# Two transformer blocks on one core: the last expert group's down pieces cut by output half, the PLE gate product begun on one half, and the latent products of the second mixer in rounded parts

## The chip, the core and the metric

The program runs on one core of a Trainium2 chip. The core has TensorE (PE, matmuls into PSUM; PEld is its weight load), VectorE (DVE), ScalarE (ACT), GpSimd (POOL), SyncE (SP, which here only issues DMAs) and 16 DMA engines. Each engine runs its own list of instructions in order; they meet at semaphores. The metric is the time of one execution on the device, in microseconds, and the median of some runs stands for a kernel. Lower is better.

## What is computed

256 tokens of width 1024 pass through two blocks. The first is a mixer and a convolutional MLP. The second is what the change is about:

```python
def second_block(x, p, ...):
    h = _rmsnorm(x, norm_mix_g)
    c_q, c_kv, k_r, x_m, z, i_pre, f_pre = _split_in(h @ w_in)
    q = (_rmsnorm(c_q, q_norm_g) @ w_uq)        # 256 -> 8 heads x 96
    kv = (_rmsnorm(c_kv, kv_norm_g) @ w_ukv)    # 128 -> 8 heads x (64 + 64)
    attn_out = _mla_attention(...)
    xc = silu(_causal_conv(x_m, conv_w, conv_b))
    mq, mk, mv = ...                            # per-head products of xc, xc and x_m
    hm = _mlstm_chunkwise(mq, mk, mv, ig, fg)   # gates from i_pre and f_pre, scanned over time
    ml_out = (norm(hm) + ml_skip * xc) * silu(z)
    x = x + concat([attn_out, ml_out]) @ w_o
    x = x + _hier_moe(_rmsnorm(x, norm_ffn_g), ...)  # 32 experts, top 2 of one group of 8
    hp = _rmsnorm(x, norm_ple_g)
    x = x + (p @ w_ple) * sigmoid(hp @ w_ple_gate)
    return _rmsnorm(x, final_norm_g)
```

An expert is `(silu(x @ w_g) * (x @ w_u)) @ w_d` with an inner width of 256.

## The kernel before

**Exact products.** A product in full float32 is one `pe.matmul`, which the trace records as two. Elsewhere both operands are cut into a rounded high part (ACT casts it) and a rounded remainder (one subtraction), and `product` (L1853) issues three matmuls: high by high, high by low, low by high.

**The second mixer.** PE first turns the normed rows (`turn_h`, L1840) and multiplies them by the 424 columns of the latents and gates (L2122, float32). Then come four column tiles of x_m and, after the transposes of the latents (`cT`), of the rope terms and of the gates, four of z (`tiles`, L2128, rounded parts, 24 matmuls a tile). The high parts of z come from ACT (L962), the remainders from POOL (L676). The gate rows are scanned on DVE (L1502 to L1505) on 4 partitions. PE turns and spreads them (L2168), then makes q from the latents (L2180, float32), k (L2188) and v (L2194), then mq (L2209) and the attention scores (L2221). In the meantime DVE makes the four convolutions of x_m (L1514 to L1518), the weights' arguments (L1527, L1529) and the turned half of q (L1536). ACT evacuates q, k and v and rounds the eight pieces of w_o (L943) between them; POOL lowers those pieces (L685). The second half of w_o is loaded only when z is done, since it takes the panel's place (L539, semaphore `zw_used`). The raw latent weights lie in `W`; chunk 0 of the expert weights is loaded to `spare` before they are used.

**The experts.** 32 experts go in 8 groups of 4. Each group has six chunks of 2 MB, four of up weights and two of down weights, which SP loads to a ring of 12 places in the order of use; a place is loaded again when PE has used it. Per group (`pe_step`) PE gathers tokens (L2426), makes the up product (L2442), puts the rows of the step before back to their tokens (`scatter`, L2448, four matmuls a token block: two output halves, high and low), turns the activation (L2489) and makes the down product (L2502). A down chunk holds one half of the inner width for both output halves (banks 2 and 3), so both halves are complete only with the second chunk. After the last group come `last_scatter`, the two gate panels of 2 MB each, `turn_x(4, ...)` (L2363), the gate product for half 0 of block 0 in float32 (`gate_full`, L2549) and three more in rounded parts (`gate_product`). ACT and DVE close: sigmoid, product, sum, norm, store.

## Time and profile before

| | us |
|---|---|
| median of 3 runs (673.68 to 674.1) | 673.91 |
| the profiled execution | 672.95 |
| its span in the trace | 671.1 |
| PE busy | 628.6 (94%) |
| DVE busy | 377.3 (56%) |
| ACT busy | 279.6 (42%) |
| the chain that ended last: PE, DMA | 70%, 18% |

The span is what the trace covers; 1.85 us of the profiled execution lie around it. Busy shares are means over stages that have different limits: up to some 530 us PE is nearly always busy, from there to 632 us PE waits for weights again and again, and after the last chunk the DMA engines fall idle. The mean granted clock of PE is 0.985 of full speed.

### The profile page before, as it was taken

The numbers are of one execution on the slowest core, as the hardware profiler recorded it, in microseconds if no ns is written. First come the engines' busy times: TensorE is split into PE (matmuls) and PEld (weight loads), VectorE is DVE, ScalarE is ACT, GpSimd is POOL, SyncE is SP. The second block draws the span as 40 slices with busy tenths as digits, with TensorE's granted clock in tenths as the row PEclk, the third lists the DMA queues.
The fourth block names the chain that finished last, engine by engine and source line by source line (L and its number), as shares of the span: only waits on it lengthen the run. The fifth ranks groups of instructions, "written<-read, shape, count | busy, mean of one in ns | idle before, by whom it ended". The sixth has DMA issues, their size and how long they took to land.

```text
span 671.1 us, 11002 instructions
## 1 busy us (share of the span) xinstructions
PE 628.6 (94%) x4299; PEld 478.6 (71%) x4299; DVE 377.3 (56%) x665; ACT 279.6 (42%) x434; POOL 55.7 (8%) x82
## 2 busy tenths in 40 slices
PE   8999999999999999999999999999999986768895
PEld 5999998889999999996796888644444432325364
DVE  5596967587677777776777465542233221203195
ACT  6764375566555555556946721311101100010193
POOL 3000000300000000200093600000000000000010
PEclk9999999999999999999999999999999998898998
DMA  8933542777655555204923658999899999999931
GB/s 328 371 136 135 201 133 68 270 259 236 212 188 188 188 187 183 69 1 161 390 92 126 211 194 303 370 426 430 352 432 427 428 424 430 426 425 427 406 124 63
DMA packets 54604, 174.81 MB, mean 260 GB/s; under 512 B 4774, under 2 KB 29474, under 8 KB 48162
## 3 DMA queue, kind: packets, MB, share of 16 engines
q1 hardware_dynamic: 53888, 172.54, 67.3%
q10 hardware_dynamic: 674, 1.69, 0.7%
q8 instruction: 30, 0.49, 0.3%
q14 instruction: 12, 0.10, 0.0%
HBM read 173.17 MB, written 1.05 MB: 260 GB/s over the span
## 4 chain that ended last, share of the span: by engine, by line
PE 70%; DMA 18%; DVE 5%; ACT 4%; issue 2%; ACTq 0%; another core or an unknown queue 0%; POOLq 0%; POOL 0%; DVEq 0%; PEldq 0%
PE ps L1855 15%; PE ps L1857 14%; PE ps L1856 14%; DMA spare<-in_w_moe_dram 7%; DMA W<-in_w_moe_dram 7%; PE ps L2442 6%; PE ps L2426 3%; PE ps L2502 3%; PE ps L2448 2%; PE ps L2122 2%; DMA W<-in_w_in_dram 2%; DMA W<-in_w_o_dram 1%; PE ps L2549 1%; PE ps L2270 1%; DMA arena<-in_conv_ffn_dram 1%
## 5 line engine op out<-in xcount | busy, mean ns | idle before, releaser
L1855 PE MATMUL ps<-hT_high,w_up_parts 128*128 128x256 f32 x320 | 90.8, 284 | 0.0
L1857 PE MATMUL ps<-hT_high,w_up_parts 128*128 128x256 f32 x320 | 90.6, 283 | 0.0
L1856 PE MATMUL ps<-hT_low,w_up_parts 128*128 128x256 f32 x320 | 90.5, 283 | 0.0
L1344 DVE TENSOR_TENSOR w_up_parts<-W,w_up_parts 128x1024 fp32r<-128x1024 f32 x44 | 52.4, 1222 | 22.7 <-ACT w_up_parts L848 22.7
L1855 PEld LDWEIGHTS ps<-hT_high,w_up_parts 128*128 128x128 f32 x320 | 61.4, 192 | 0.5
L1856 PEld LDWEIGHTS ps<-hT_low,w_up_parts 128*128 128x128 f32 x320 | 61.4, 192 | 0.4
L1857 PEld LDWEIGHTS ps<-hT_high,w_up_parts 128*128 128x128 f32 x320 | 61.4, 192 | 0.0
L1038 ACT ACTIVATE sg<-ps 128x256 f32<-128x256 f32 x9 | 3.5, 384 | 121.1 <-PE ps L2442 121.1
L2442 PE MATMUL ps<-W,junk 128*32 128x512 f32 x368 | 46.1, 629 | 7.5 <-DMA W<-in_w_moe_dram 7.5
L848 ACT CAST w_up_parts<-W 128x1024 fp32r<-128x1024 f32 x44 | 44.5, 1048 | 20.4 <-PE ps L1857 20.4
L1855 PE MATMUL ps<-h_high,dense_high 128*128 128x256 f32 x160 | 45.8, 286 | 0.6 <-DVE dense_low L1219 0.4
L1856 PE MATMUL ps<-h_low,dense_high 128*128 128x256 f32 x160 | 45.3, 283 | 0.0
L1857 PE MATMUL ps<-h_high,dense_low 128*128 128x256 f32 x160 | 45.2, 283 | 0.0
L2426 PEld LDWEIGHTS ps<-arena,x_tok 128*128 128x128 f32 x288 | 35.3, 204 | 11.0 <-issue 11.0
L1367 DVE SCALAR_TENSOR_TENSOR arena<-ps,arena 128x255 f32<-128x255 f32 x80 | 33.1, 476 | 17.2 <-ACT arena L884 16.9
L2426 PE MATMUL ps<-arena,x_tok 128*128 128x128 f32 x288 | 36.9, 290 | 3.1 <-DVE arena L1712 2.0
L1219 DVE TENSOR_TENSOR dense_low<-W,dense_high 128x1024 fp32r<-128x1024 f32 x31 | 36.0, 1218 | 2.7 <-ACT dense_high L777 2.6
L777 ACT CAST dense_high<-W 128x1024 fp32r<-128x1024 f32 x30 | 29.4, 1044 | 13.0 <-PE ps L1857 10.0
L2442 PEld LDWEIGHTS ps<-W,junk 128*32 128x32 f32 x368 | 10.7, 112 | 31.1 <-issue 20.7
L1855 PE MATMUL ps<-w_down_high,uact_high 128*128 128x512 f32 x80 | 31.4, 392 | 0.9 <-DVE uact_low L1378 0.9
L1855 PEld LDWEIGHTS ps<-h_high,dense_high 128*128 128x128 f32 x160 | 30.6, 192 | 2.0 <-issue 1.5
L1856 PE MATMUL ps<-w_down_low,uact_high 128*128 128x512 f32 x80 | 31.3, 391 | 0.0
(491 smaller groups left out, 1346.6 us busy)
## 6 DMA issues: line engine op xcount, KB each, us to landing
W<-in_w_moe_dram SPq DMA_DIRECT2D x22, 2048.0 KB, 21.1
arena<-in_w_moe_dram SPq DMA_DIRECT2D x14, 2048.0 KB, 30.1
W<-in_w_up_dram SPq DMA_DIRECT2D x22, 1024.0 KB, 8.2
W<-in_w_in_dram SPq DMA_DIRECT2D x7, 2048.0 KB, 10.4
W<-in_w_down_dram SPq DMA_DIRECT2D x11, 1024.0 KB, 4.9
spare<-in_w_moe_dram SPq DMA_DIRECT2D x5, 2048.0 KB, 20.7
hh<-in_w_moe_dram SPq DMA_DIRECT2D x4, 2048.0 KB, 33.1
W<-in_w_out_dram SPq DMA_DIRECT2D x2, 2048.0 KB, 8.7
```

Of the source, the lines that this page charges most:

```text
L777: act.copy(piece(panel_hl(n)[0], n, c), piece(panel(n), n, c)).then_inc(sig("dense_high"), 1)
L848: act.copy(w_up_hl[0][:, c], U[q][:, :, g, i * P:(i + 1) * P]).then_inc(sig("up_high"), 1)
L1219: dve.tensor_tensor(piece(panel_hl(n)[1], n, c), piece(panel(n), n, c), piece(panel_hl(n)[0], n, c).bitcast(F32), ALU.subtract).then_inc(s ...
L1344: dve.tensor_tensor(w_up_hl[1][:, c], U[q][:, :, g, i * P:(i + 1) * P], w_up_hl[0][:, c].bitcast(F32), ALU.subtract).then_inc(sig("up_low" ...
L1367: dve.scalar_tensor_tensor(o, s, w, o, ALU.mult, ALU.add).then_inc(sig("tap_done"), 1)
L1855: pe.matmul(o, lhs[0], rhs[0], start=first, stop=False, skip_group_check=True)
L1856: pe.matmul(o, lhs[0], rhs[1], start=False, stop=False, skip_group_check=True)
L1857: return pe.matmul(o, lhs[1], rhs[0], start=False, stop=last_k, skip_group_check=True)
L2122: last = pe.matmul(ps[:, 2 + b, 0:424], hT[:, k, b * P:(b + 1) * P], wA[:, k, :], start=(k == 0), stop=(k == KD - 1))
L2426: last = pe.matmul(ps[:, h, (k % 4) * P:(k % 4 + 1) * P], x_tok[:, b, k * P:(k + 1) * P], hot[:, b, :], start=(b == 0), stop=(b == 1))
L2442: last = pe.matmul(ps[CAP * c:CAP * c + CAP, 2, :], xg[:, k, CAP * c:CAP * c + CAP], up_chunk(CPG * g + j)[:, c, kk, :], start=(k == 0), s ...
L2502: last = pe.matmul(ps[CAP * c:CAP * c + CAP, bank, :], aT[:, f, CAP * c:CAP * c + CAP], down_chunk(CPG * g + UPC + f)[:, c, 512 * half:512 ...
```

## The change

**Last group and gate.** The host lays the down weights out anew: each of the two down chunks of a group now holds one output half for the whole inner width. All groups compute one half, then the other (`down_half`), and ACT rounds the first half's rows after the first chunk. In the last group the first half is put back to its tokens before the last quarter of the down product (`scatter_half`, twice: for the rows of the step before it stands ahead of the last group). The last chunk is loaded in two parts of 1 MB, cut by inner half, and the first gate panel too, with rows 4 to 7 of its eight first; the gate weights are laid out in one piece. The gate product of block 0 begins on the turned rows of half 1 (k = 4 to 7) while half 0 is put back. Ten short matmuls (`keep_sharp`) stand in the last group in place of five of 512 columns.

**Second mixer.** The latents and their weights are rounded (ACT, four casts) and lowered (DVE, four subtractions), and q, k and v use `product`. The remainders of z move from POOL to DVE. The gate rows are turned, and half of them spread, between the third and the fourth tile of z. The convolutions are cut in two pairs around the weights' arguments. POOL starts the pieces of w_o after the last convolution. Chunk 0 is loaded later, with chunk 1, since `spare` now holds rounded weights.

**End of the first MLP.** POOL instead of DVE lowers one of the last down pieces; the down products of the last pairs stand in another order, the last one of the first token block two products further ahead; DVE evacuates two turned halves earlier in the hand-over; 6 of 10 filler matmuls go.

```diff
@@ SP
-            load_chunk(0)
             sp.wait_ge(sig("a2_used"), 1)
             sp.dma_start(PAN[5], w_o[:, :, 512:1024]).then_inc(sig("wo1_landed"), 16)
...
             sp.wait_ge(sig("uq_used"), 1)
+            load_chunk(0)
             load_chunk(1)
...
+                elif n == NCHUNK:
+                    sp.dma_start(ring(n)[:, 0:UNIT // 2], w_moe[NGRP8 - 1, CPG - 1][:, 0:UNIT // 2]).then_inc(sig("last_landed"), 16)
+                    sp.dma_start(ring(n)[:, UNIT // 2:UNIT], w_moe[NGRP8 - 1, CPG - 1][:, UNIT // 2:UNIT])\
+                        .then_inc(sig(f"ring{n % RING}_landed"), 16)
+                elif n == NCHUNK + 1:
+                    sp.dma_start(wpg[0][:, 4:KD, :], w_gate[0, :, 4:KD, :]).then_inc(sig("gate_landed"), 16)
+                    sp.dma_start(wpg[0][:, 0:4, :], w_gate[0, :, 0:4, :]).then_inc(sig(f"ring{n % RING}_landed"), 16)
@@ POOL
-            for c in range(4):
-                o = (slice(None), slice(None), slice(c * P, c * P + P))
-                pool.wait_ge(sig("dense_high"), 32 + 4 + c + 1)
-                pool.tensor_tensor(z_low[o], PAN[1][o], proj_high[:, c].bitcast(F32), ALU.subtract).then_inc(sig("dense_rest"), 1)
...
+            pool.wait_ge(sig("conv2_late"), at("conv2_late", 2))
             for n, (h, q) in enumerate(WO_PARTS):
@@ ACT
+            act.wait_ge(sig("cT_ready"), at("cT_ready", 2))
+            act.copy(cT_hl[0], cT).then_inc(sig("ct_high"), 1)
+            act.wait_ge(sig("uq_landed"), at("uq_landed", 32))
+            for j in range(3):
+                raw, high, _ = latent_piece(j)
+                act.copy(high, raw).then_inc(sig("lat_high"), 1)
             round_out(WO_PARTS[0:2])
...
+            for n in range(2):
+                conv, xc, qn = (("conv2_done", "xc_ready", "qn_ready"), ("conv2_late", "xc_late", "qn_late"))[n]
+                for h in (2 * n, 2 * n + 1):
+                    act.wait_ge(sig(conv), at(conv, h - 2 * n + 1))
+                    act.activation(xcT[:, h, :], xcT[:, h, :], ACT.Silu, bias=par_c("conv_b_2", h)).then_inc(sig(xc), 1)
+                for hp in (2 * n, 2 * n + 1):
+                    act.wait_ge(sig("qa_done"), at("qa_done", hp + 1))
+                    act.mul(qTa[0:64, 2 * hp:2 * hp + 2, :], v3(ps[0:64, hp, :], 2), A_SCALE).then_inc(sig(qn), 1)
+                    if hp < 3:
+                        round_out(WO_PARTS[2 + hp:3 + hp])
@@ PE
-            keep_busy(0, 4)
+            keep_busy(0, 3)
             turn_h(2, 0)
-            keep_busy(3, 6)
+            keep_busy(3, 1)
...
+            tiles(z_low, (2, 3), "dense_rest", 0, ("z2_done", "z2_late"), turn_gates)
+            pe.wait_ge(sig("z2_late"), at("z2_late", 1))
+            pe.sem_inc(sig("zw_used"), 1)
+            spread_max(1)
...
-                        last = pe.matmul(ps[:, hp, 256 * hh:256 * hh + 256], uq[:, k, h * P:(h + 1) * P], cT[:, k, :],
-                                         start=(k == 0), stop=(k == 1))
+                        last = product(ps[:, hp, 256 * hh:256 * hh + 256], [t[:, k, h * P:(h + 1) * P] for t in uq_hl],
+                                       [t[:, k, :] for t in cT_hl], k == 0, k == 1)
...
+            def expert_down(n, g):
+
+                pe.wait_ge(sig("aT_ready"), n + 2)
+                down_half(n, g, 0).then_inc(sig("downw_used"), 1)
+                if g < NGRP8 - 1:
+                    down_half(n, g, 1).then_inc(sig("downw_used"), 1)
+                    return
+                pe.wait_ge(sig("sc_ready"), n + 2)
+                keep_sharp(6)
+                down_half(n, g, 1, (0,))
+                scatter_half(n + 1).then_inc(sig("half_back"), 1)
+                keep_sharp(4)
+                down_half(n, g, 1, (1,)).then_inc(sig("downw_used"), 1)
...
+            turn_ple(1)
+            pe.wait_ge(sig("ypa_ready"), begun + 1)
+            for b in range(TB):
+                slots_back(b, 0, False)
+            turn_ple(3)
+            gate_full(4)
+            pe.wait_ge(sig("yl_ready"), begun * 2 + 2)
+            for b in range(TB):
+                slots_back(b, 0, True).then_inc(sig("moe_done"), 1)
+            gate_full(5)
+            gate_full(6)
+            turn_ple(0)
+            gate_full(7)
+            turn_ple(2)
+            for k in range(3):
+                gate_full(k)
+            gate_full(3).then_inc(sig("pg_done"), 1)
@@ DVE
...
+            dve.wait_ge(sig("half_back"), at("half_back", rounds))
+            for b in range(TB):
+                dve.tensor_copy(x_tok[:, b, 512:D], ps[:, 5 + 2 * b, :]).then_inc(sig("x_ready"), 1)
+            turned_ple(1)
+            lower_slots(0, begun)
+            turned_ple(3)
+            dve.wait_ge(sig("moe_done"), 1)
+            dve.tensor_copy(x_tok[:, 0, 0:512], ps[:, 4, :]).then_inc(sig("x_ready"), 1)
+            lower_gate(2)
+            turned_ple(0)
...
```

On PE at the end of the last group, before: `hh` and `spare` hold the two down chunks, `sg` the activation, `slots_high` and `slots_low` the rounded rows, `scatter_rows` the map back to the tokens; a count stands for matmuls alike in a row.

```order
L2502 MATMUL ps<-hh,sg 32x512 x8
L2498 MATMUL ps<-slots_high 128x512 x5
L2502 MATMUL ps<-spare,sg 32x512 x8
L2536 REGISTER_ALU
L2536 COMPARE_AND_BRANCH
L2538 TENSOR_LOAD arena
L2538 ISA x2
L2463 REGISTER_ALU
L2448 MATMUL ps<-slots_high,scatter_rows 128x512 x4
L2470 ISA
L2448 MATMUL ps<-slots_low_67,scatter_rows 128x512
```

There, after:

```order
L2585 MATMUL ps<-hh,sg 32x512 x8
L2606 MATMUL ps<-scatter_rows 128x256 x6
L2585 MATMUL ps<-spare,sg 32x512 x4
L2536 MATMUL ps<-slots_high,scatter_rows 128x512 x2
L2557 ISA
L2536 MATMUL ps<-slots_low_67,scatter_rows 128x512 x2
L2606 MATMUL ps<-scatter_rows 128x256 x4
L2585 MATMUL ps<-spare,sg 32x512 x4
```

Eight matmuls on the last chunk have become four and four, with the rows of one half put back between them. Behind them PE had the 4 turns, the last rows back and the gate product one after the other; now 4 turns of half 1, the rows of half 0 and single gate matmuls alternate.

On DVE in the second mixer, from the transposed latents (L1494) to the first convolution (L1514), before; the four rows on 4x256 are the scan of the gates:

```order
L1494 TENSOR_TENSOR arena<-ps,par 128x3x128 x2
L1498 COPY arena<-ps 64x256
L1499 COPY arena<-ps 64x256
L1500 COPY arena<-ps 4x512
L1502 SCALAR_TENSOR_TENSOR arena<-arena 4x256
L1503 TENSOR_TENSOR arena<-arena 4x256
L1504 SCALAR_TENSOR_TENSOR arena<-arena 4x256
L1505 TENSOR_TENSOR arena<-arena 4x256
L1514 TENSOR_SCALAR arena<-arena,par 128x256
L1516 SCALAR_TENSOR_TENSOR arena<-arena,par 128x256 x2
```

There, after:

```order
L1530 TENSOR_TENSOR z_low<-W,proj_high 128x8x128 x2
L1537 TENSOR_TENSOR arena<-ps,par 128x3x128 x2
L1530 TENSOR_TENSOR z_low<-W,proj_high 128x8x128
L1542 COPY arena<-ps 64x256
L1543 COPY arena<-ps 64x256
L1544 COPY arena<-ps 4x512
L1530 TENSOR_TENSOR z_low<-W,proj_high 128x8x128
L1547 SCALAR_TENSOR_TENSOR arena<-arena 4x256
L1548 TENSOR_TENSOR arena<-arena 4x256
L1549 SCALAR_TENSOR_TENSOR arena<-arena 4x256
L1550 TENSOR_TENSOR arena<-arena 4x256
L1553 TENSOR_TENSOR cT_low<-arena,cT_high 128x768
L1557 TENSOR_TENSOR latent_low<-W,latent_high 128x2x512 x2
L1557 TENSOR_TENSOR latent_low<-W,latent_high 128x1024
```

The four subtractions of z stand around the evacuations, and the four of the latents between the scan and the convolutions.

## Rows read from the trace of the kernel before

**Rows 1.** windows: busy us by engine, granted clock, DMA share, GB/s of stretches.

```profile
368.10:380.30 12.20, 11.79 (x75) 10.13 (x73) 5.95 (x13) 10.55 (x18) 8.91 (x4) 1.00 0.48 174
...
478.00:480.00 2.00, 2.00 (x24) 0.52 (x16) 0.00 (x0) 0.00 (x0) 0.00 (x0) 1.00 0.60 139
...
490.00:500.00 10.00, 10.00 (x90) 5.47 (x90) 3.76 (x7) 1.07 (x2) 0.00 (x0) 1.00 1.01 429
...
570.00:580.00 10.00, 8.93 (x64) 5.33 (x64) 3.33 (x6) 1.07 (x2) 0.00 (x0) 0.83 1.00 426
...
636.00:638.00 2.00, 1.68 (x8) 0.94 (x7) 1.41 (x3) 1.02 (x3) 0.00 (x0) 1.00 1.06 388
```

**Rows 2.** the chain that ended last: start us, us, what.

```profile
352.94 8.89 DMA W<-in_w_o_dram
...
583.81 48.65 DMA spare<-in_w_moe_dram
```

**Rows 3.** timeline, PE, 312 to 339 us: start, us, line, names, [idle before].

```profile
312.23 1.09 PE L1850 MATMUL ps<-ident,hh 128*128 128x128 f32 x8 [0.91 <-DVE hh L1191]
...
314.46 4.50 PE L2122 MATMUL ps<-W,hh 128*128 128x424 f32 x12
...
327.35 0.36 PE L1855 MATMUL ps<-h_high,proj_high 128*128 128x256 f32 x1 [0.40 <-PE ps L2122]
...
338.93 0.82 PE L2144 MATMUL ps<-ident,arena 128*128 128x128 f32 x6
```

**Rows 4.** timeline, PE, the second mixer, 353 to 371 us.

```profile
353.36 1.97 PE L2168 MATMUL ps<-arena 4*128 4x256 f32 x8
...
355.26 7.17 PE L2180 MATMUL ps<-arena,W 128*128 128x256 f32 x32
...
363.01 3.67 PE L2188 MATMUL ps<-arena,W 128*64 128x256 f32 x16 [0.58 <-DVE arena L1529]
...
370.81 5.40 PE L2221 MATMUL ps<-arena 128*128 128x128 f32 x32
```

**Rows 5.** timeline, DVE and then POOL, 342 to 353 us.

```profile
342.85 2.89 DVE L1502 TENSOR_TENSOR_SCAN arena<-arena 4x256 f32<-4x256 f32 x1
...
350.34 2.45 DVE L1505 TENSOR_TENSOR arena<-arena 4x256 f32<-4x256 f32 x1
...
347.30 5.21 POOL L685 TENSOR_TENSOR wo_low<-W,wo_high 128x1024 fp32r<-128x1024 f32 x2
```

**Rows 6.** groups by line, DVE: names, shapes, count | busy us, mean ns.

```profile
L1241 DVE TENSOR_TENSOR_SCAN arena<-arena 128x512 f32<-128x512 f32 x1 | 1.2, 1226 | 0.0
...
L1219 DVE TENSOR_TENSOR dense_low<-W,dense_high 128x1024 fp32r<-128x1024 f32 x31 | 36.0, 1218 | 2.7 <-ACT dense_high L777 2.6
```

**Rows 7.** timeline, ACT, 361 and 380 us.

```profile
361.85 1.04 ACT L943 CAST wo_high<-W 128x1024 fp32r<-128x1024 f32 x1 [0.74 <-DMA W<-in_w_o_dram]
...
380.31 0.75 ACT L1001 CAST nm<-ps 8x256 fp32r<-8x256 f32 x2
```

**Rows 8.** timeline, PE, last group and gate products, from 627 us.

```profile
627.80 1.92 PE L2502 MATMUL ps<-hh,sg 128*32 128x512 f32 x16
...
632.50 1.92 PE L2502 MATMUL ps<-spare,sg 128*32 128x512 f32 x16 [1.42 <-DMA spare<-in_w_moe_dram]
...
635.22 1.18 PE L2448 MATMUL ps<-slots_high,scatter_rows 128*128 128x512 f32 x4 [0.80 <-ACT slots_high L1042]
...
639.26 3.67 PE L2549 MATMUL ps<-W,hh 128*128 128x512 f32 x8 [0.44 <-DVE hh L1639]
...
643.64 3.60 PE L2549 MATMUL ps<-W,hh 128*128 128x512 f32 x8
...
646.68 0.79 PE L1855 MATMUL ps<-wpg_high,hpT_high 128*128 128x512 f32 x1
...
663.20 0.39 PE L1857 MATMUL ps<-wpg_high,hpT_low 128*128 128x512 f32 x1
```

**Rows 9.** timeline, DVE, near the end of the program.

```profile
664.40 0.69 DVE L1811 TENSOR_TENSOR arena<-arena 128x512 f32<-128x512 f32 x1 [1.77 <-ACT arena L1078]
```

More of the change, by code:

```diff
@@ L1759, in _ @@
                 if g == NGRP8 - 1:
+                    lower_slots(1, begun)
                     for q in range(4):
@@ L1838, in _, with turn_h @@
             keep_busy(4, 6)
-            def turn_h(r, b):
-                for h in range(2):
+            def turn_h(r, b, halves=range(2)):
+                for h in halves:
                     j = 2 * b + h
@@ L2126, in _, with tiles @@
             pe.sem_inc(sig("a2_used"), 1)
-            def tiles(low, banks, ready, base, signal):
+            def tiles(low, banks, ready, base, signals, between=None):
                 for h in range(2):
@@ L2187, in _ @@
                     h = 2 * hp + hh
-                    last = pe.matmul(ps[0:NOPE, 4 + hp, 256 * hh:256 * hh + 256], ukv[:, h * P:h * P + NOPE], cT[:, 2, :],
-                                     start=True, stop=True)
+                    last = product(ps[0:NOPE, 4 + hp, 256 * hh:256 * hh + 256], [t[:, h * P:h * P + NOPE] for t in ukv_hl],
+                                   [t[:, 2, :] for t in cT_hl], True, True)
                 last.then_inc(sig("ka_done"), 1)
@@ L2563, in _ @@
[L2563 to L2569 removed]
+                        pe.wait_ge(sig("y1_low"), 7 + HP_ORDER.index(2 * b + k // 4) + 1)
+                    last = product(ps[:, 5 + 2 * b - half, :], [t[:, k, b * P:(b + 1) * P] for t in hpT],
+                                   [wpg_high[half][:, k, :], wpg_low[half][:, k, :]], k == ks[0], k == ks[-1])
```

424 lines of the change are left out of this document (236 added, 188 removed).

## The prediction, made before the changed kernel was run

> **What bounds the kernel now.** I read the chain of waits first, then the windows, then the timelines at the places where the chain changes hands. The chain ends with the weight stream: the load of the last chunk to `spare` (48.65 us in a full queue, landed at 632.5) and then 38.6 us of work behind it up to the end of the span at 671.1 [rows 2, 8]. Before the stream the chain runs through the second mixer, and there it holds the load of half of w_o, 8.89 us from 352.94, which can start only when z is done [rows 2]. In between lie the groups. The windows say who leads there: at 478 to 480 us PE is busy all the time and the DMA share falls to 0.60, since the ring is full and SP waits for a place; from 490 us on the share is 1.01 [rows 1]. So the stream restarts when PE frees a place near 479 us and is full from then on: what the mixer gains or loses before that point moves the stream, and with it the landing at 632.5, one for one. What happens on PE between 490 and 627 us moves nothing. The sum therefore has two parts: the mixer's exit, and the work behind the last landing.
>
> **The change, part by part. 1, the way into the mixer.** Two products of the last down stage are moved behind the last one of token block 0. A rounded matmul of 512 columns takes 0.233 us (71 steps from 646.68 to 663.20) [rows 8], so this block's result comes 6 x 0.233 = 1.4 us earlier, less 0.2 us in which PE now waits for the activation remainder of DVE: 1.2. The b0 turns stood waiting on DVE until 312.23 [rows 3] and go to 311.1. Between their end (1.09 us later) and the first latent product at 314.46 stood six fillers; with one, the product can start when DVE has evacuated the first half, about 0.2 us after the turns, at 312.4. The 16 latent products and the other turns are as many as before, so the x_m tiles start at 325.3 for 327.35: **2.0 us earlier**. Cover: the rounding of x_m must be ready at 325.3; ACT and DVE do it in the same order from rows that are turned 1 us earlier, so some tenths may be lost.
>
> **2, the gates.** On DVE the scan's four rows reach from 342.85 to 350.34 + 2.45 = 352.8, 9.9 us. A scan over 512 columns takes 1.2 us elsewhere [rows 6], here one over 256 takes 2.89, and a subtraction of 256 columns 2.45 [rows 5]. The last subtraction starts inside POOL's two pieces of w_o and ends at 352.8, just after they do at 347.30 + 5.21 = 352.5. I read this as DVE held up until POOL's instruction is over. Without a neighbour the four take about 2 x 0.65 + 2 x 0.3 = 1.9 us (an estimate: half of 1.2 each for the scans). The change takes POOL's pieces away until the convolutions are done and adds 4 x 1.22 us of z on DVE [rows 6], of which two stand in an idle stretch, one behind the turned latents, and the last before the scan, where it may wait for POOL's copy. I get gates at 345.2; PE asks for them after the third z tile at 347.7. Cover 2.5 us. If the 9.9 us stay, they come after 352 and PE stands some 2 to 5 us with a z tile behind the wait.
> In the Trainium skill, page SBUF — State Buffer, section SBUF: two separate sides, the pair of ports that VectorE and GpSimd share is an exclusive lock for a whole instruction, also for a VectorE operation with two SBUF inputs against GpSimd. The rows agree, but the rule cuts the other way too. The eight w_o pieces (2.6 us each, half of 5.21 [rows 5]) now run in one row after the last convolution, over the small minimum behind the scores; by the rule it can wait up to 2.6 us, and the sum would then end 0 to 1.5 us worse.
>
> **3, q, k and v.** A rounded matmul of 256 columns takes (338.93 - 327.35) / 96 = 0.121 us [rows 3]. For q 32 records of 7.17 us become 48 x 0.121 = 5.8; for k 3.67 becomes 24 x 0.121 = 2.9 [rows 4]; for v two float32 products of 512 columns (0.92 each, as 3.67 for four [rows 8]) become 6 x 0.233 = 1.4. Together 2.6 us less PE. The price: three casts of 1.04 and a smaller one on ACT [rows 7], and about 4.6 us on DVE (3.8 x 1.22) ahead of the convolutions. DVE has them done at 349.6 and the first two convolutions at 353.3, for 356.4 in the old order.
>
> **4, where that gain goes.** z ends at 350.9 + 1.0 (turning and half of the 1.97 us of spreading [rows 4] now stand in it) = 352.0, so the w_o half is asked for 0.95 us earlier, and q starts at 352.9 for 355.26: 2.35 earlier. q ends at 358.75, k at 361.7. But ACT, in order, rounds a w_o piece after its first share of q. It waited 0.74 us for the load at 361.85 [rows 7]; now it waits there from 355.0 to 360.9. Behind it stand the second share of q (v waits for it), two more convolutions' silu, two pieces, the other q and k: about 7.4 us, to 368.3. The scores need k from ACT, so they start at 368.3 for 370.81 [rows 4]: 2.5 earlier, with PE idle some 3 us in between. From there ACT has the same list as before and no idle time left: between 368.1 and 380.3 it was busy for 10.55 of 12.2 us [rows 1], so 1.6 us idle, and the row maxima's cast at 380.31 [rows 7], on which the next step hangs, stands at the end. So that point moves by 1.3 us only. **The mixer's exit: 1.3 us earlier.** Bounds: 2.5 if ACT's list lies beside the path after all; a loss of 0.9 if the gates keep their 9.9 us, by the same walk. I take 1.3 since that is what the busiest queue allows. The later load of chunk 0 costs nothing: two chunks are 10 us from 364, and SP asks for the next only at about 378.
>
> **5, behind the last landing.** L is the landing, 632.5. Before: down 1.92, wait 0.80, four rows back high (1.18) and four low, turns, two float32 halves of 3.67 and 3.60 at 639.26 and 643.64, then 72 rounded matmuls from 646.68, which is L + 14.2 [rows 8]. After: only a quarter of the down product needs the last megabyte, 0.96. Rows back of half 1 (four of eight, 1.1) are done before L; PE is at 632.3 with them if the first megabyte comes 2.4 us before the second (half of the 4.9 us that a chunk takes at 429 GB/s [rows 1]). What remains before the 72: 0.96 + two pairs of rows back 1.1 + four turns of 0.5 + float32 7.3 = 11.4, and the waits for ACT and DVE now have a turn or a gate matmul beside them; the gate panel's first half must be there at L + 2.4, asked for at L + 3. So they start at L + 11.4 to 11.6: 2.7 us earlier on PE, at most 3.1. DVE is the second limit: its eight remainders of the gate (9.8 us), four of the turned rows and the evacuations fill it until about L + 20.4, and PE's last two products need them at a distance of 0 to 0.2 us. The closing chain hangs on DVE's row at 664.40, which waited 1.77 us [rows 9]; I get it at 661.6. **2.8 us earlier.** Bounds: 1.0 if the parts do not land ahead (then only the rows back of half 1 leave the path), 3.4 if every wait goes. The gate weights in one piece should also lift the 388 GB/s at 636 to 638 [rows 1] towards 429, which nobody waits for.
>
> **The sum.** 671.1 - 1.3 - 2.8 = 667.0 for the span, 672.95 - 4.1 = 668.85 for the profiled execution. That one lies 0.96 under the median of 673.91, and I carry the difference: 673.91 - 4.1 = **669.8 us**.
>
> **Rivals.** *A, the mixer gives nothing* (ACT's list, or 0.5 us here and there): for it speak 3 us of new idle time on PE and a load that ACT must wait for 5.9 us; 671.1. *B, both give all*: 2.5 and 3.4, 668.0. *C, the change does not do what it says at the end*: the first part of the last chunk lands with the second, since both lie in one full queue on 16 engines; then PE waits for it, and the tail gives 1.0: 671.6, or 672.9 with a mixer that gives nothing. *D, slower, by the clock.* PE ran at 0.83 mean in 570 to 580, at work for 8.93 of 10 us and waiting for DMA [rows 1]; that is the 1.2 GHz level for a third of the time. After the change PE works in shorter pieces between waits behind L, and the fillers are shorter. If the clock falls to 1.2 GHz for all of the float32 gate part, its 7.3 us become 14.6 and the time 677. It decides from 4.1 us on, more than half of that part. Against it: 1.00 at 636 to 638, where PE worked 1.68 of 2 us [rows 1].
> The Trainium skill, TensorE: Matmul & The Clock Gate, section HAM oscillation, has it that matmuls in bursts between waits for DMA fall back to the lower level again and again. By it D would be likelier than I hold it.
>
> **Chances.** Forecast (668.9 to 670.8) 0.50; A 0.22; B 0.12; C 0.10, of which 0.06 within 0.2% of the old time; D 0.04; the rest lies between. 0.2% is 1.35 us, about what a measurement of this kernel can tell from no change. The range of 8 in 10 takes in B and A and the better half of C: 667.8 to 672.2. Faster 0.90, same 0.06, slower 0.04.
>
> **What would show it.** In the new trace: the x_m tiles start near 325.3; the four scan rows take about 2 us; q starts near 352.9; the scores near 368.3, the row maxima's cast near 379.0; the last down quarter starts where its DMA ends, near 631.2 (L itself moved by 1.3); the first rounded gate matmul 11.5 us after it for 14.2. The prediction is wrong if the stream is not tied to PE near 479 us (then the tail alone shows), if PE stands before the last z tile, or if the granted clock is under 0.95 after the last landing.

## The result, and the profile after

The changed kernel takes 668.3 us (median of 4 runs, 667.8 to 668.4), for 674.0 us before in the same series. The ratio is 0.992 (95% interval 0.990 to 0.993): 5.7 us less. The profiled execution took 668.31 us with a span of 666.6, for 672.95 and 671.1 before. So the two profiles differ by 4.6 us and the medians by 5.7; the forecast was 4.1 for both. Two of the eight executions of `pool_back`, an experiment below, were in a much slower state (1027 and 1568 us) and are left out of its ratio.

The load of the w_o half still stands on the chain of waits, about where it stood [rows 2]. The last load on the chain is now that of the first down chunk (`hh`), since the last chunk no longer holds PE up:

```profile
352.84 8.97 DMA W<-in_w_o_dram
...
581.33 44.65 DMA hh<-in_w_moe_dram
```

PE's timeline from the mixer's entry to the scores answers to [rows 3, 4]; start us, us, line, names, idle time before:

```profile
325.77 0.36 PE L1930 MATMUL ps<-h_high,proj_high 128*128 128x256 f32 x1 [0.30 <-PE ps L2198]
...
348.28 0.41 PE L2249 MATMUL ps<-ident,arena 4*128 4x4 f32 x4
348.55 1.10 PE L2238 MATMUL ps<-arena 4*128 4x256 f32 x4
...
352.87 1.10 PE L2238 MATMUL ps<-arena 4*128 4x256 f32 x4
...
369.08 5.48 PE L2309 MATMUL ps<-arena 128*128 128x128 f32 x32 [0.87 <-ACT arena L1012]
```

The x_m tiles start 1.58 us earlier than in [rows 3], the scores 1.73 us earlier than in [rows 4]. The gate rows on DVE, which reached from 342.85 to 352.8 [rows 5], are over in 2.3 us:

```profile
343.32 0.67 DVE L1547 TENSOR_TENSOR_SCAN arena<-arena 4x256 f32<-4x256 f32 x1
344.03 0.41 DVE L1548 TENSOR_TENSOR arena<-arena 4x256 f32<-4x256 f32 x1
344.47 0.68 DVE L1549 TENSOR_TENSOR_SCAN arena<-arena 4x256 f32<-4x256 f32 x1
345.19 0.41 DVE L1550 TENSOR_TENSOR arena<-arena 4x256 f32<-4x256 f32 x1
```

ACT's timeline answers to [rows 7]. It stands at the w_o half for 5.60 us where it stood for 0.74, and it goes on at the same time, 361.83 for 361.85. Yet the row maxima's cast comes 1.64 us earlier, because ACT has no idle time left behind the load (1.6 us of it before, in five waits for PE between 371 and 380 us):

```profile
355.63 0.59 ACT L1007 ACTIVATE arena<-ps 64x512 f32<-64x512 f32 x1 [1.49 <-PE ps L1932]
361.83 1.05 ACT L969 CAST wo_high<-W 128x1024 fp32r<-128x1024 f32 x1 [5.60 <-DMA W<-in_w_o_dram]
...
366.92 2.02 ACT L1012 COPY arena<-ps 64x512 f32<-64x512 f32 x4
...
378.67 0.74 ACT L1035 CAST nm<-ps 8x256 fp32r<-8x256 f32 x2
```

The two parts of the last chunk, by the view of one tile (issue, then the least, median and longest time to landing), land at 582.38 + 46.1 = 628.5 and 594.09 + 36.8 = 630.9. The second is the landing L, 1.6 us earlier than before:

```profile
L602 SPq DMA_DIRECT2D spare<-in_w_moe_dram x1: 11670/11670/11670, 582.4 to 582.4; - x1
L603 SPq DMA_DIRECT2D spare<-in_w_moe_dram x1: 2404/2404/2404, 594.1 to 594.1; - x1
...
DMA to landing us min/median/max: 36.8/41.5/46.1
```

PE at the close, and DVE's row that waited at 664.40 before [rows 8, 9]:

```profile
628.87 1.06 PE L2585 MATMUL ps<-spare,sg 128*32 128x512 f32 x8
...
630.90 0.64 PE L2606 MATMUL ps<-scatter_rows 128*128 128x256 f32 x4
631.46 1.07 PE L2585 MATMUL ps<-spare,sg 128*32 128x512 f32 x8
...
642.04 0.80 PE L1930 MATMUL ps<-wpg_high,hpT_high 128*128 128x512 f32 x1
...
659.86 0.69 DVE L1886 TENSOR_TENSOR arena<-arena 128x512 f32<-128x512 f32 x1
```

The first rounded gate product stands at L + 11.1 (L + 14.2 before), the end of the span at L + 35.7 (L + 38.65 before). PE's granted clock is 1.00 from 630 to 645. The gate panels move at 429 and 442 GB/s (631 to 634 and 634 to 637 us), where it had been 388 [rows 1].

### The profile page after: what moved, and what is told of

Read it like the earlier page. It is cut to its first block, busy times and chain, and to the rows that moved or that the text cites. A ratio compares the mean times of both kernels' runs of the same rounds, so it can differ in the third digit from the quotient of the medians.

```text
span 666.6 us, 11072 instructions
## 1 busy us (share of the span) xinstructions
PE 623.8 (94%) x4324; PEld 476.4 (71%) x4324; DVE 379.3 (57%) x673; ACT 282.1 (42%) x437; POOL 48.8 (7%) x79
## 4 chain that ended last, share of the span: by engine, by line
PE 62%; DMA 17%; DVE 8%; ACT 7%; SPq 3%; issue 2%; ACTq 0%; POOLq 0%; POOL 0%; DVEq 0%; PEldq 0%
PE ps L1930 13%; PE ps L1932 13%; PE ps L1931 13%; DMA hh<-in_w_moe_dram 7%; DMA W<-in_w_moe_dram 6%; PE ps L2530 6%; PE ps L2514 3%; PE ps L2585 3%; SPq L553 3%; PE ps L2198 2%; DMA W<-in_w_in_dram 2%; PE ps L2536 2%; DMA W<-in_w_o_dram 1%; PE ps L2358 1%; DMA arena<-in_conv_ffn_dram 1%
## 5 line engine op out<-in xcount | busy, mean ns | idle before, releaser
L874 ACT CAST w_up_parts<-W 128x1024 fp32r<-128x1024 f32 x44 | 44.5, 1048 | 20.3 <-PE ps L1932 20.3
L2514 PEld LDWEIGHTS ps<-arena,x_tok 128*128 128x128 f32 x288 | 32.8, 192 | 8.4 <-issue 8.4
L2514 PE MATMUL ps<-arena,x_tok 128*128 128x128 f32 x288 | 34.4, 278 | 1.5 <-ACT x_tok L1060 0.9
## 6 DMA issues: line engine op xcount, KB each, us to landing
W<-in_w_in_dram SPq DMA_DIRECT2D x7, 2048.0 KB, 10.7
```

Source lines behind the costliest of these rows:

```text
L874: act.copy(w_up_hl[0][:, c], U[q][:, :, g, i * P:(i + 1) * P]).then_inc(sig("up_high"), 1)
L2514: last = pe.matmul(ps[:, h, (k % 4) * P:(k % 4 + 1) * P], x_tok[:, b, k * P:(k + 1) * P], hot[:, b, :], start=(b == 0), stop=(b == 1))
```

## Milestones of all runs

The experiments are read by five points of each trace. The profiled executions differ by up to 0.8 us before anything of the change is reached (the first block's turns on PE start between 114.2 and 115.0), so distances say more than times. A distance has a spread of its own: five kernels with the same mixer code (after, tail_mixer, no_fillers, one_piece, filler_late) have mixers of 52.54 to 53.13. "Mixer" is from the first x_m tile to the row maxima's cast, "stream" from there to L, "tail" from L to the span's end. Ratios are to the kernel before of the same series.

| kernel | x_m tiles | mixer | stream | tail | span | ratio (interval) |
|---|---|---|---|---|---|---|
| before | 327.35 | 52.96 | 252.1 | 38.7 | 671.1 | |
| after | 325.77 | 52.90 | 252.2 | 35.7 | 666.6 | 0.992 (0.990 to 0.993) |
| tail_only | 327.58 | 54.00 | 252.5 | 35.6 | 669.7 | 0.996 (0.995 to 0.998) |
| tail_mixer | 327.72 | 52.72 | 252.0 | 35.7 | 668.1 | 0.994 (0.993 to 0.995) |
| latents_f32 | 325.63 | 52.54 | 252.4 | 35.7 | 666.3 | 0.992 (0.991 to 0.994) |
| wo_behind | 326.06 | 50.01 | 252.5 | 35.8 | 664.4 | 0.987 (0.986 to 0.989) |
| gates_behind | 325.40 | 52.74 | 252.3 | 35.6 | 666.0 | 0.990 (0.988 to 0.991) |
| pool_back | 325.51 | 60.80 | 253.1 | 35.6 | 675.0 | 1.004 (1.003 to 1.006) |
| before_again | 327.46 | 52.95 | 252.1 | 38.7 | 671.2 | |
| no_fillers | 325.55 | 53.04 | 252.5 | 35.2 | 666.3 | 0.990 (0.988 to 0.992) |
| one_piece | 325.58 | 53.13 | 252.2 | 39.4 | 670.3 | 0.996 (0.994 to 0.997) |
| filler_late | 325.26 | 52.54 | 252.1 | 35.8 | 665.7 | 0.992 (0.990 to 0.993) |
| both_f32 | 325.97 | 52.59 | 252.2 | 35.7 | 666.5 | 0.992 (0.991 to 0.993) |
| best | 325.41 | 49.99 | 252.2 | 35.2 | 662.8 | 0.987 (0.986 to 0.989) |

The stream's column is the first finding: over exits that range from 375.4 to 386.3 it stays at 252.0 to 253.1 (252.0 to 252.5 without `pool_back`). What the mixer gains or loses reaches the landing nearly one for one.

## The experiments

**The change in its parts.** `tail_only` is the kernel before with the expert weights' layout, the last group and the gate product of the change; `tail_mixer` has the second mixer's edits too. What is then missing to the changed kernel is the end of the first MLP. These lines, from the changed kernel to `tail_mixer`, show the order of the down products and the fillers:

```diff
...
-            down_before(1, 0, range(1))
+            down_before(1, 0, range(2))
+            down_before(1, 1, range(1))
             down_last(0, 1).then_inc(sig("y_done"), 1)
...
-            keep_busy(0, 3)
+            keep_busy(0, 4)
             turn_h(2, 0)
-            keep_busy(3, 1)
+            keep_busy(3, 6)
...
```

> The kernel before with the change of the last group, of the expert weights' layout and of the gate product alone; mixer and first MLP as before. Theory (two separate parts, the second is the work behind the last landing): the last chunk lands where it did, near 632.4, the first rounded gate product comes about 11.2 us behind it (14.2 before), the span is 671.1 - 2.9 = 668.2, the ratio to before 0.9957. Rival (the tail needs the earlier mixer, or the extra microsecond by which the medians moved more than the two profiled executions lies in the tail): span 669.5 or more in the one case, ratio 0.994 in the other.

> The changed kernel with the end of the first MLP and the hand-over to the second mixer as before (fillers, order of the last down products, DVE lowering both pieces). Theory (the mixer's exit hangs on the end of z, the load of the w_o half behind it and ACT's list behind that load, so it keeps only what z's end keeps): x_m tiles at 327.35, z's end and the load 1.5 us later than in the changed kernel (352.84), the cast of the row maxima at 380.2 (378.67 in the changed kernel, 380.31 before); the mixer's own edits then give 0.1 us and the time is that of tail_only within 0.3 us. Rival (the mixer's own edits give most of the 1.64 us and the earlier start the rest, as the forecast had it that DVE's and PE's savings count by themselves): cast at 379.3 or earlier, 1 us or more under tail_only.

Measured: medians 671.5 us and 669.9 us, for 674.0 before and 668.3 after. The tail is 3.0 to 3.1 us shorter in both, as in the changed kernel: it needs nothing of the mixer. That part of the theory holds, but the span of `tail_only`, 669.7, is on the rival's side (669.5 or more), for a reason that neither had named: 1.0 us in its mixer, below. In `tail_mixer` the mixer takes 52.72 us for 52.96 before. ACT's timeline there shows why: the load is later by the tiles' later start, the wait is as long as in the changed kernel, and the cast is back at its old place.

```profile
363.60 1.05 ACT L966 CAST wo_high<-W 128x1024 fp32r<-128x1024 f32 x1 [5.45 <-DMA W<-in_w_o_dram]
...
380.44 0.74 ACT L1032 CAST nm<-ps 8x256 fp32r<-8x256 f32 x2
```

So by the traces the mixer's own edits gave next to nothing (52.54 to 53.13 in the five kernels that have them, 52.95 and 52.96 in the two traces of the kernel before), the MLP's end 1.8 us (first x_m tile against the turns at 114 us: 212.9 before, 211.1 after), the tail 3.0 us. The medians don't divide like that: from `tail_only` to `tail_mixer` they fall by 1.6 us, where the theory had 0.3 at most and only the rival 1 or more, although the cast, at 380.44, is the theory's (380.2) and not the rival's (379.3). The windows of `tail_only` (us, busy of PE, PEld, DVE, ACT, POOL, granted clock, DMA share, GB/s) show what is missing:

```profile
352.00:356.00 4.00, 3.69 (x23) 2.92 (x23) 3.82 (x8) 1.10 (x2) 0.74 (x1) 0.97 0.36 97
356.00:360.00 4.00, 4.00 (x13) 3.24 (x12) 3.75 (x10) 1.02 (x2) 0.00 (x0) 0.61 1.05 400
```

Its mixer is the code of before, and yet takes 54.00 us for 52.96: the clock fell to about the 1.2 GHz level for some 3 us, just behind the turned and spread gates, and q got slower. I come back to that under `gates_behind`.

**Do the rounded latents pay?** `latents_f32` makes q, k and v from the raw weights again and drops the four casts and the four remainders:

```diff
...
-                        last = product(ps[:, hp, 256 * hh:256 * hh + 256], [t[:, k, h * P:(h + 1) * P] for t in uq_hl],
-                                       [t[:, k, :] for t in cT_hl], k == 0, k == 1)
+                        last = pe.matmul(ps[:, hp, 256 * hh:256 * hh + 256], uq[:, k, h * P:(h + 1) * P], cT[:, k, :],
+                                         start=(k == 0), stop=(k == 1))
...
```

> The changed kernel with q, k and v made in float32 from the raw latents again, no casts and remainders for them. Theory (ACT's list behind the w_o load sets the exit, PE has idle time there): PE busy 2.6 us more between 352 and 369, the cast of the row maxima stays within 0.2 us of 378.67, the time within 0.3 us of the changed kernel (668.3). Rival (q, k and v lie on the path): exit and time 1.5 to 2.6 us later, 670 to 671.

Measured: 668.05 us (one of its five executions took 670.27), ratio 0.992, mixer 52.54 us for 52.90. The windows of 352 to 369 us, first of this kernel, then of the changed one:

```profile
352.00:369.00 17.00, 16.44 (x73) 11.72 (x73) 7.61 (x16) 9.64 (x18) 6.72 (x3) 1.00 0.47 145
```

```profile
352.00:369.00 17.00, 14.38 (x96) 12.07 (x95) 10.46 (x25) 9.15 (x17) 7.12 (x3) 1.00 0.51 178
```

In this stretch PE has 2.06 us more work (2.6 were expected) and 2.06 us less idle time, and nothing behind it gets later: the cast comes at 378.17 for 378.67. In the changed kernel the rounded latents are worth nothing.

**The wait that takes it.** `wo_behind` lets ACT round the late pieces of w_o behind what PE waits for:

```diff
...
-                for hp in (2 * n, 2 * n + 1):
-                    act.wait_ge(sig("qa_done"), at("qa_done", hp + 1))
-                    act.mul(qTa[0:64, 2 * hp:2 * hp + 2, :], v3(ps[0:64, hp, :], 2), A_SCALE).then_inc(sig(qn), 1)
-                    if hp < 3:
-                        round_out(WO_PARTS[2 + hp:3 + hp])
+            silu_conv(0)
+            for hp in range(4):
+                act.wait_ge(sig("qa_done"), at("qa_done", hp + 1))
+                act.mul(qTa[0:64, 2 * hp:2 * hp + 2, :], v3(ps[0:64, hp, :], 2), A_SCALE).then_inc(sig(("qn_ready", "qn_late")[hp // 2]), 1)
+            silu_conv(1)
...
                 act.wait_ge(sig("mq_done"), at("mq_done", h + 1))
                 act.copy(mqT[:, 2 * h:2 * h + 2, :], v3(ps[:, 2 + h, :], 2)).then_inc(sig("mq_ready"), 1)
+            round_out(WO_PARTS[2:4])
...
```

> The changed kernel with ACT's roundings of the w_o pieces moved behind the evacuations: q, k, v and mq first, then two pieces, the exponentials, two pieces, and the last two behind the cast of the row maxima. Theory (the exit hangs on ACT standing at the load of w_o until 361.83 with q and k behind it): no such wait ahead of k, scores near 366.0 for 369.08, cast of the row maxima at 376.5 to 377, time 1.7 to 2.2 us under the changed kernel, 666.3. Rival (something else, DVE's maxima, POOL's lowering of w_o or a load, is 0.5 us behind): the cast moves by 0.5 at most, or it moves and the stream does not, 667.8 to 668.3.

`both_f32` is the same with q, k and v in float32:

> wo_behind with q, k and v in float32 from the raw latents, as in latents_f32. Theory (once ACT no longer stands at the w_o load, PE's own list sets the exit, and the 2.6 us of the rounded latents are on the path; in the changed kernel they were not): cast of the row maxima 2 to 2.6 us later than in wo_behind (376.07), time 667.6 to 668.1 for 665.45. Rival (DVE's convolutions or maxima set the exit of wo_behind, and DVE has 4.6 us less here): within 0.5 us of wo_behind or under it.

Measured: `wo_behind` 665.45 us, ratio 0.987. `both_f32` 668.06 us, ratio 0.992 in a series in which the kernel before took 673.1. The mixers take 50.01 and 52.59 us. ACT in `wo_behind`, with no wait for the load in it:

```profile
358.80 0.59 ACT L1010 ACTIVATE arena<-ps 64x512 f32<-64x512 f32 x1 [0.85 <-PE ps L1935]
360.23 0.59 ACT L1010 ACTIVATE arena<-ps 64x512 f32<-64x512 f32 x1 [0.84 <-PE ps L1935]
...
362.28 2.01 ACT L1014 COPY arena<-ps 64x512 f32<-64x512 f32 x4
...
367.21 1.99 ACT L969 CAST wo_high<-W 128x1024 fp32r<-128x1024 f32 x2
...
376.07 0.74 ACT L1037 CAST nm<-ps 8x256 fp32r<-8x256 f32 x2
```

ACT now waits for PE. The scores start at 366.52 and the mixer is 2.9 us shorter. The float32 latents, free of charge a moment ago, now cost 2.58 us. The edit and the wait cover each other: rounding pays only once ACT's order is changed, and with float32 latents the changed order gives nothing (52.59 for 52.54).

**The gates between the tiles.** `gates_behind` moves the turned and spread gate rows behind the four z tiles, so that z ends, and w_o is asked for, earlier:

```diff
-            tiles(z_low, (2, 3), "dense_rest", 0, ("z2_done", "z2_late"), turn_gates)
+            tiles(z_low, (2, 3), "dense_rest", 0, ("z2_done", "z2_late"))
             pe.wait_ge(sig("z2_late"), at("z2_late", 1))
             pe.sem_inc(sig("zw_used"), 1)
+            turn_gates()
```

> The changed kernel with the gate rows turned and spread behind the four z tiles again instead of between the third and the fourth; DVE, ACT and POOL as changed. Theory (the exit hangs on z's end by way of the w_o load and ACT's list): z ends and the load starts 1.5 us earlier (351.3 for 352.84), the cast of the row maxima comes at 377.3 for 378.67, the time is 1.3 us less, 667.0, although PE does the same work. The four transposes and eight small spreads on 4 partitions then stand in one row again just ahead of q; if PE's granted clock falls there, as in the one execution of tail_only (0.61 in 356 to 360), up to 1.3 us of it is lost again in such executions. Rival (PE's own list is the path): exit unchanged within 0.2 us, 668.3.

Measured: 667.4 us, ratio 0.990, but in two groups: spans of 664.7 and 665.2, and of 666.0 and 666.7. The profiled one is of the second. PE, then ACT, then PE's clock there:

```profile
351.15 0.38 PE L2249 MATMUL ps<-ident,arena 4*128 4x4 f32 x4 [0.30 <-PE ps L1932]
351.39 2.32 PE L2238 MATMUL ps<-arena 4*128 4x256 f32 x8
```

```profile
359.93 1.05 ACT L969 CAST wo_high<-W 128x1024 fp32r<-128x1024 f32 x1 [2.72 <-DMA W<-in_w_o_dram]
```

```profile
354.00:360.00 6.00, 6.00 (x31) 6.00 (x31) 3.51 (x10) 0.67 (x2) 0.00 (x0) 0.52 0.70 268
```

The load came 1.9 us earlier (1.5 of it by the edit, since this execution was 0.4 us ahead), and the two shorter spans are 1.4 and 1.9 us under 666.6. So the theory holds for the load by this trace. For the time it holds by the two shorter executions, of which there is no trace; against the kernel before of its own series the median of `gates_behind` has gained 6.7 us, the changed kernel's 5.7. In the profiled execution the clock was at 1.2 GHz for nearly all of 354 to 360, and the gain was lost in q. PE had been idle for 0.3 us only; it had made 2.6 us of small matmuls on 4 partitions. The mean granted clock of an execution is 0.987 in both shorter executions, 0.978 and 0.981 in the longer ones, which fits a fall in those two alone.

With half of the spreads between the tiles no trace (of ten kernels) has a clock below 1.00 in 345 to 365 us. With all of them behind z it has in two of four traces: `tail_only` and `gates_behind`, not the two of the kernel before. The other executions of the kernel before have spans of 670.6 to 672.6, more than half of them near 672, though both profiled ones have 671.1 and 671.2. That such falls make up the missing 1 us of the medians is the best account I have, but it is not shown: no trace of the kernel before has one. For it speaks that the spans of one kernel range over 2.0 to 2.3 us in all three kernels with the old place of the gates (four, five and, for the kernel before, some thirty executions), and over 0.2 to 1.2 us in seven of the ten with the new one (`pool_back` has 3.0, `one_piece` 2.0, `latents_f32` one of five that is 2.1 us longer). Against it: the mean granted clock does not part the long executions of the kernel before (0.976 to 0.988 near 672) from the short ones (0.982 to 0.987 near 671).

> The kernel before, unchanged, for the profile of another execution. Its nine timed executions have spans of 671.4 to 672.3, the profiled one 671.1. Theory (in most executions the granted clock falls for a few us just behind the gates' small matmuls at 353 us, as in tail_only, and not in the one that was profiled): a window of 352 to 364 us with a clock of 0.6 to 0.9, the cast of the row maxima 0.5 to 1.3 us later than 380.31, the last chunk landed as much later than 632.45. Rival: the clock is 1.00 there and a longer span has its excess elsewhere (a late landing in the stream or the tail).

Measured: a span of 671.2, a clock of 1.00 in 345 to 365 us, the cast at 380.41. This was one of the short executions, as the first profiled one was, and it shows no fall. What the long ones lose stays open.

**POOL and DVE.** `pool_back` gives z's remainders back to POOL and lets it lower w_o at once:

```diff
...
+            for c in range(4):
+                o = (slice(None), slice(None), slice(c * P, c * P + P))
+                pool.wait_ge(sig("dense_high"), 32 + 4 + c + 1)
+                pool.tensor_tensor(z_low[o], PAN[1][o], proj_high[:, c].bitcast(F32), ALU.subtract).then_inc(sig("dense_rest"), 1)
...
-            pool.wait_ge(sig("conv2_late"), at("conv2_late", 2))
             for n, (h, q) in enumerate(WO_PARTS):
...
```

> The changed kernel with the remainders of z on POOL again and the w_o pieces lowered as soon as they are rounded; DVE makes none of z's. Theory (DVE's rows with two SBUF operands stand still while POOL's instruction runs): the four gate rows take about 10 us again (2.2 in the changed kernel, 9.9 before) and end near 351; PE waits some 5 us for them after the third z tile, the w_o load starts near 354.3 for 352.84, q waits for the latents' remainders until 355 to 356, the exit and the time come about 1.5 to 2 us later, 670. Rival (the long rows came from something else, as the shape on 4 partitions or the waits between them): four rows in 2.2 us, time within 0.3 us of 668.3.

Measured: 675.2 to 678.3 us in six executions, slower than before, ratio 1.004, span 675.0, mixer 60.80 us. The direction is the theory's, the size is not: I had expected 670. DVE and then POOL and PE in `pool_back`:

```profile
342.62 2.46 DVE L1548 TENSOR_TENSOR arena<-arena 4x256 f32<-4x256 f32 x1
...
364.25 5.14 DVE L1570 SCALAR_TENSOR_TENSOR arena<-arena,par 128x256 f32<-128x256 f32 x2
```

```profile
346.70 9.39 POOL L715 TENSOR_TENSOR wo_low<-W,wo_high 128x1024 fp32r<-128x1024 f32 x2
...
364.23 4.89 POOL L715 TENSOR_TENSOR wo_low<-W,wo_high 128x1024 fp32r<-128x1024 f32 x2 [8.13 <-ACT wo_high L973]
```

```profile
372.86 3.75 PE L2297 MATMUL ps<-arena,W 128*128 128x256 f32 x8 [5.90 <-ACT arena L1011]
```

The four gate rows take 8.6 us (about 10 expected), and PE waits 1.58 us for them, not 5. The larger price stands at 364: two rows of the third convolution that take 1.00 us elsewhere take 5.14, about as long as POOL's two pieces (4.89) that started 0.02 us before them, and q's last shares on ACT and mq on PE stand behind them. It goes both ways: POOL's first two pieces take 9.39 us for 5.21 in [rows 5]. Rows of DVE that read PSUM are not touched: the turned halves of q take 1.30 us for two in the changed kernel beside POOL at 361.6, and 1.33 without it at 356.4.

The Trainium skill, page SBUF — State Buffer, section SBUF: two separate sides, calls this an exclusive lock for a whole instruction, also against VectorE with two SBUF inputs. The rows agree. What I had feared from the same rule, the small minimum behind the scores, took 0.56 us in the changed kernel beside a busy POOL, and 0.17 in a gap of POOL in `wo_behind`. The fear was right in kind: beside a busy POOL the same row took between 0.30 us (`one_piece`) and 2.31 us (`pool_back`, where POOL's piece had started 0.08 us before it). The changed kernel's 0.56 is where its row happened to meet the end of a piece.

**The last chunk.** `one_piece` loads it as a whole:

```diff
...
-                    sp.dma_start(ring(n)[:, 0:UNIT // 2], w_moe[NGRP8 - 1, CPG - 1][:, 0:UNIT // 2]).then_inc(sig("last_landed"), 16)
-                    sp.dma_start(ring(n)[:, UNIT // 2:UNIT], w_moe[NGRP8 - 1, CPG - 1][:, UNIT // 2:UNIT])\
-                        .then_inc(sig(f"ring{n % RING}_landed"), 16)
+                    load_chunk(n)
...
```

> The changed kernel with the last chunk loaded in one piece of 2 MB; both quarters of the last down product wait for it. Theory (the parts land 2.4 us apart, and the first quarter with the rows back of half 1 is hidden ahead of the landing): PE stands until 630.9, then makes the quarter, four rows back, the fillers and the second quarter, which starts at 633.5 for 631.46; everything behind it and the time are 2.0 us later, 670.3. Rival (C of the forecast, the parts land together and the split brings nothing): time within 0.3 us of the changed kernel, 668.3.

Measured: spans of 668.3 (twice), 669.6 and 670.3, ratio 0.996. PE in the profiled one, and its window:

```profile
630.98 1.35 PE L2580 MATMUL ps<-spare,sg 128*32 128x512 f32 x8 [1.98 <-DMA spare<-in_w_moe_dram]
...
635.11 1.06 PE L2580 MATMUL ps<-spare,sg 128*32 128x512 f32 x8
```

```profile
630.00:636.00 6.00, 5.02 (x24) 2.56 (x24) 1.29 (x2) 0.00 (x0) 0.00 (x0) 0.72 1.02 427
```

The second quarter starts 3.65 us later than in the changed kernel, where 2.0 were expected: behind a wait of 1.98 us the clock fell, and the quarter, the rows back and the fillers took 1.3 to 1.7 times as long. The two shorter spans, 1.7 us over 666.6, are near the 2.0 of the split alone; they have no trace. So C is refuted, and the mechanism of D exists: here it struck where PE waited ahead of the landing, a wait that the split chunk has taken away. It need not strike: the kernel before waited 1.42 us at this place [rows 8], and its clock is 1.00 from 631 to 637.

The Trainium skill, page TensorE: Matmul & The Clock Gate, section HAM oscillation, says that matmuls between waits for DMA fall back to the lower level. `one_piece` agrees for its wait of 1.98 us; the next kernel, with waits of 0.55 and 0.21 us at the same place, shows no fall.

**The fillers.** `no_fillers` drops `keep_sharp(6)` and `keep_sharp(4)`:

```diff
-                keep_sharp(6)
                 down_half(n, g, 1, (0,))
                 scatter_half(n + 1).then_inc(sig("half_back"), 1)
-                keep_sharp(4)
                 down_half(n, g, 1, (1,)).then_inc(sig("downw_used"), 1)
```

> The changed kernel without the ten short filler matmuls in the last group. Theory (the second part of the last chunk lands at 630.9 and PE is held until 631.46 by the four fillers alone): PE starts on the last quarter at about 631.0, everything behind it 0.4 to 0.5 us earlier, 667.9. Rival (the fillers hold PE's clock, D of the forecast): the granted clock behind the last landing falls below 1.00 and the float32 gate matmuls take 0.9 instead of 0.45 us each for a while; time 670 or more.

Measured: 667.6 us, ratio 0.990, tail 35.2 us for 35.7. PE now waits for the landing and not for its own fillers, and the clock stays at 1.00 behind it:

```profile
628.72 1.06 PE L2585 MATMUL ps<-spare,sg 128*32 128x512 f32 x8 [0.55 <-DMA spare<-in_w_moe_dram]
...
631.11 1.07 PE L2585 MATMUL ps<-spare,sg 128*32 128x512 f32 x8 [0.21 <-DMA spare<-in_w_moe_dram]
```

`filler_late` does the reverse where PE waits for the stream:

```diff
                 down_half(n, g, 0).then_inc(sig("downw_used"), 1)
+                if g in (4, 5, 6):
+                    pe.wait_ge(sig("sc_ready"), n + 2)
+                    keep_sharp(18)
```

> The changed kernel with 18 more short filler matmuls (2 us of PE) in each of the groups 4, 5 and 6, between about 515 and 600 us, 6 us more work on PE in all. Theory (from 490 us on the stream is full, PE only waits for it): the last chunk lands at 630.9 as in the changed kernel, PE waits less, the time stays within 0.3 us of 668.3. Rival (PE leads there too, or frees ring places late): 2 to 6 us later.

Measured: 667.4 us, ratio 0.992. The windows of 515 to 605 us, first of the changed kernel, then of this one:

```profile
515.00:605.00 90.00, 69.55 (x494) 29.45 (x487) 17.85 (x34) 7.72 (x16) 0.00 (x0) 0.94 1.01 427
```

```profile
515.00:605.00 90.00, 77.18 (x542) 36.11 (x535) 18.25 (x35) 7.71 (x16) 0.00 (x0) 0.92 1.01 427
```

PE is busy 7.6 us longer (6 were expected), the stream takes 252.1 us for 252.2. This much work on PE there is free.

**Both together.** `best` is `wo_behind` without the fillers.

> wo_behind without the ten fillers of the last group: two places that do not touch. Theory: the gains add, 665.45 - 0.7 = 664.8 (no_fillers took 0.75 us from the median of the changed kernel, 0.5 us by its trace). Rival (the fillers matter for the clock at another distance of the landings): granted clock below 1.00 behind the last landing, 666 or more.

Measured: 664.5 us (664.47 to 664.59, 4 runs), ratio 0.987. That is 3.8 us under the changed kernel's 668.3, which was timed in another series; in its own series `filler_late`, which does what the changed kernel does and adds only work that is free, took 667.4, so 2.9 us. By the trace the gains add: the mixer (49.99) and the tail (35.2) are those of the two parts, and the clock behind the landing is 1.00. The times do not show it as clearly: `best` lies 8.6 us under the kernel before of its series, `wo_behind` 8.5 under that of its own, and the two series differ by 0.9 us in the kernel before, more than the 0.5 to 0.7 us that were to be added.

## Why the prediction came out as it did

**The mechanism** was right in both parts and in what joins them. The stream follows the mixer's exit, the work that was added on PE between 515 and 605 us is free, and the second part is a fixed list behind the landing. Two of its sizes and the last line of the sum were not right, as follows.

**The way in.** Forecast 2.0 us, measured 1.58, or 1.8 if each execution is counted from its own 114 us. The first latent products started at 312.94 where I had 312.4.

**The gates.** Forecast ready at 345.2 on DVE, measured 345.6; PE took them at 348.28, without a wait. The reading that DVE's rows stand still beside POOL was right. I had priced it at 2 to 5 us of waiting on PE for the gates; in `pool_back` that wait is 1.58 us, but the mixer is 7.9 us longer, since the convolutions hang on it too.

**z's end and the load.** This size was the furthest off in the mixer. I let z end at 352.0 and the load start 0.95 us earlier; it started 0.1 us earlier (352.84 for 352.94). The tiles began 0.4 us later than in my walk, and turning plus half of the spreads took 1.5 us inside z, not 1.0; q started at 353.89 for 352.9. I had priced the delay of the load by the gates at 1.0 us and taken it for worth having, as a gain for q. `gates_behind` shows 1.5 us at the load, and by its two shorter executions 1.4 to 1.9 us of the time.

**ACT's list.** The claim that it swallows the 2.6 us of the rounded latents was right: `latents_f32` is as fast. Its size was off the other way. From the load's landing to the cast I had 18.1 us, the trace has 16.8: 0.8 of that because the list from where the scores start ran without a gap in 9.9 us for my 10.7, the rest ahead of them. That this error and the late load nearly cancelled is luck: exit forecast 1.3 us earlier, measured 1.64.

**The tail.** Forecast 2.8, measured 3.0; the first rounded product at L + 11.1 for L + 11.4 to 11.6; the parts land 2.4 us apart, as forecast. DVE ended its remainders at L + 20.3 for L + 20.4.

**The carried difference.** Of the 1.5 us between 669.8 and 668.3, 0.5 are these sizes, and 1.0 is the last line of the sum. I carried the 0.96 us by which the profiled execution of before lay under its median. This term had no reason but that the difference was there, and it failed: after the change the profiled execution lies at the median. So the gap was not a constant of the measurement. Most executions of the kernel before lose time somewhere that the profiled one did not. The falls of the clock behind the gates are a candidate, seen in two kernels with the old place of the gates and not in the kernel before; the cause stays open.

**The rivals.** The measured 668.3 lies within the range of 8 in 10, below the forecast's own band of 668.9 to 670.8. A (the mixer gives nothing) is refuted for the time and true of the mixer's own edits; what arrived came from the MLP's end. B (668.0) was nearest to the measured time, but not for its own reason: the exit gave 1.64 us and not 2.5, the tail 3.0 and not 3.4, and the rest is the carried difference. C is refuted by `one_piece`. D did not happen in the changed kernel; the trace of `one_piece` has such a fall behind a wait of 1.98 us.

## What to carry to other kernels

When an edit makes an engine's work shorter, look for the in-order queue behind which its result is read: here ACT stood at a load for 5.6 us with q, k and v behind it. Making q, k and v cheaper gave nothing as long as it did, moving six casts that nobody waited for gave nothing with q, k and v in float32, and both together gave 2.9 us. Price a moved step by what it holds back as well as by what it frees; the gates between the tiles held back a load. And if a profiled execution lies away from its median, don't carry the difference into a forecast without a reason: here the change took it away, and what it was made of is still open.

## What the runs showed of the hardware

- The granted clock can fall with PE hardly idle: 0.52 over 6 us behind 2.6 us of matmuls on 4 partitions with 0.3 us idle ahead of them (`gates_behind`), 0.61 over 4 us behind the same work in `tail_only`. The two traces of the kernel before have the same work at this place and 1.00 behind it. A wait of 1.98 us was followed by 0.72 over 6 us (`one_piece`), one of 1.42 us at the same place by 1.00 (the kernel before), and so were waits of 0.55 and 0.21 us (`no_fillers`).
- The hold-up between DVE and POOL works in both directions: two rows of DVE went from 1.00 to 5.14 us, two of POOL from 5.21 to 9.39 (4.84 beside no such row, `wo_behind` at 361.96). Where a short row of DVE meets a piece of POOL decides its price: the minimum on 64x16 took 0.17 to 2.31 us.
